# The sums of squares of the recurrence heads as two fp32r products, one unit later

## The reference

```
def _rmsnorm(x, g):
    xf = x.astype(jnp.float32)
    r = lax.rsqrt(jnp.mean(xf * xf, axis=-1, keepdims=True) + EPS)
    return (xf * r).astype(x.dtype) * g

_, o = lax.scan(_hgrn2_chunk_step, s0, xs)      # q, k, g, v in chunks of 64
o = o.transpose(1, 0, 3, 2, 4).reshape(B, S, HG_HEADS, HG_DV)
o = _rmsnorm(o, norm_g) * jax.nn.silu(og.reshape(B, S, HG_HEADS, HG_DV))

y = sigmoid(gate_a) * (a @ w_br_gm) + sigmoid(gate_b) * (b @ w_br_hg)    # a: gMLP branch, b: o
x = x + y @ w_out
x = x + _conv_ffn(_rmsnorm(x, ffn_norm), w_up, conv_w, conv_b, w_down)   # up 1024 -> 5632, down 2816 -> 1024
```

## Time and profile before

| | us |
|---|---|
| median of 3 runs | 2916.29 (2916.15 to 2920.58) |
| the profiled execution's own time | 2918.32 |
| its span, first to last instruction | 2916.5 |
| PE busy in the span | 2881.0 (99%) |
| DVE, ACT, POOL busy | 1459.5 (50%), 710.1 (24%), 195.8 (7%) |
| mean granted TensorE clock | 0.998 |

### The profile page before, as it was taken

The page is one execution under the profiler, slowest core; times in us unless marked ns, Lnnn a source line. Parts: engine busy times, 40 slices in busy tenths (PEclk is TensorE's granted clock), DMA queues, the critical chain, the costliest instruction groups (busy, mean ns, idle before and its releaser), DMA issues.

```text
span 2916.5 us, 33708 instructions
## 1 busy us (share of the span) xinstructions
PE 2881.0 (99%) x13472; PEld 2397.8 (82%) x13472; DVE 1459.5 (50%) x2870; ACT 710.1 (24%) x971; POOL 195.8 (7%) x87
## 2 busy tenths in 40 slices
PE   7999999999999999999999999999999999999998
PEld 6888888888888888888888888888888888888886
DVE  2886677755266434553325634455323563355521
ACT  3332244433122112221112211222111211122210
POOL 3323410014000000000000000000000000000000
PEclk9999999999999999999999999999999999999999
DMA  7657888889743465556564445555656345555554
GB/s 269 236 184 236 316 284 293 288 304 322 253 159 132 163 224 188 190 200 229 204 217 144 145 172 218 188 193 197 231 204 215 132 143 196 208 188 197 193 204 171
DMA packets 121979, 614.61 MB, mean 211 GB/s; under 512 B 13536, under 2 KB 13792, under 8 KB 74080
## 3 DMA queue, kind: packets, MB, share of 16 engines
q1 hardware_dynamic: 121824, 612.46, 59.8%
HBM read 474.00 MB, written 138.41 MB: 210 GB/s over the span
## 4 chain that ended last, share of the span: by engine, by line
PE 93%; DMA 2%; DVE 2%; issue 1%; POOL 1%; ACT 0%; SPq 0%; POOLq 0%; DVEq 0%; ACTq 0%
PE bank L889 26%; PE bank L890 26%; PE bank L894 26%; PE bank L950 3%; PE bank L937 2%; PE bank L938 2%; PE bank L939 2%; DMA w_split<-w_both 1%; POOL w_both L384 1%; DMA raw<-w_units 1%; PE bank L903 1%; PE bank L900 1%; PE bank L901 0%; PE bank L920 0%; PE bank L991 0%
## 5 line engine op out<-in xcount | busy, mean ns | idle before, releaser
L889 PE MATMUL bank<-h_hi,w_both 128*128 128x512 f32 x2400 | 945.5, 394 | 0.0
L890 PE MATMUL bank<-h_lo,w_both 128*128 128x512 f32 x2400 | 934.3, 389 | 0.0
L894 PE MATMUL bank<-h_hi,w_both 128*128 128x512 f32 x2400 | 593.5, 389 | 0.0
L890 PEld LDWEIGHTS bank<-h_lo,w_both 128*128 128x128 f32 x2400 | 450.7, 188 | 96.9 <-issue 4.8
L889 PEld LDWEIGHTS bank<-h_hi,w_both 128*128 128x128 f32 x2400 | 450.7, 188 | 96.9 <-issue 4.8
L894 PEld LDWEIGHTS bank<-h_hi,w_both 128*128 128x128 f32 x2400 | 450.5, 188 | 93.6
L811 DVE TENSOR_TENSOR z<-bank,rms_inv 128x512 f32<-128x512 f32 x176 | 121.8, 692 | 355.3 <-PE bank L894 347.7
L889 PE MATMUL bank<-g_hi,w_both 128*128 128x512 f32 x704 | 275.4, 391 | 0.0
L890 PE MATMUL bank<-g_lo,w_both 128*128 128x512 f32 x704 | 273.9, 389 | 0.0
L824 DVE SCALAR_TENSOR_TENSOR conv<-z,params,conv 128x512 f32<-128x512 f32 x352 | 263.7, 750 | 6.2
L384 POOL TENSOR_TENSOR w_both<-raw,w_both 128x1024 fp32r<-128x1024 f32 x80 | 194.7, 2434 | 531.4 <-ACT w_both L398 504.5
(11 more groups left out here) (187 smaller groups left out, 3055.4 us busy)
## 6 DMA issues: line engine op xcount, KB each, us to landing
w_both<-w_split SPq DMA_DIRECT2D x372, 1024.0 KB, 4.8
w_split<-w_both SPq DMA_DIRECT2D x248, 512.0 KB, 5.5
raw<-w_units SPq DMA_DIRECT2D x124, 512.0 KB, 5.3
x_in<-x_t SPq DMA_DIRECT2D x32, 256.0 KB, 5.5
res<-x_t SPq DMA_DIRECT2D x32, 256.0 KB, 5.1
out<-res SPq DMA_DIRECT2D x32, 256.0 KB, 6.8
masks<-masks_in SPq DMA_DIRECT2D x1, 1152.0 KB, 9.7
gm_w<-gm_wt SPq DMA_DIRECT2D x1, 256.0 KB, 6.9
```

The source lines that it names most:

```text
L889: pe.matmul(dst, w_hi[slot][:, off + k, :], rhs_hi(k), start=first and k == 0, stop=False)
L890: pe.matmul(dst, w_hi[slot][:, off + k, :], rhs_lo(k), start=False, stop=False)
L894: mm = pe.matmul(dst, w_lo[slot][:, off + k, :], rhs_hi(k), start=False, stop=last and k == n - 1)
```

## The change

The sum of squares over the channels becomes two fp32r matmuls of `ones_r` with the two halves of the squares: ScalarE makes the upper half (`sq_hi`, a copy behind the square), VectorE the rest (`sq_lo`, behind `a_lo`). Both halves lie where `sig_nf` and `sig_q` lay. TensorE issues the two matmuls behind the first unit of the next head, for the last head behind the first unit of the gates (`o_sum`). ScalarE takes the root there: behind `sig_nf` of the next head, or ahead of the first gate's sigmoid (`o_rms`); `sig_nf` itself waits for the sum, because it writes over `sq_hi`. VectorE finishes the head's output (`recurrence_out`, the five steps that stood at the head's end) between q0 and `qp1` of the next head, for the last head behind the loop. The steps get semaphores of their own.

```diff
--- before.py
+++ after.py
@@ -134,6 +134,7 @@
     masks = place("masks", [P, NC * P + len(LEVELS) * NC * P // 2], U32)
     ident = place("ident", [P, P])
     ones = place("ones", [P, P])
+    ones_r = place("ones_r", [P, P], F32R)
     eps = place("eps", [P, 1])
     scratch = place("scratch", [P, 8])
     gm_w = place("gm_w", [P, NH, P])
@@ -181,13 +182,14 @@
     SLOT = BLK + 64
     pool = room(10 * SLOT)
 
-    def temp(name, slot, width=TT):
-        return place(name, [P, width], F32, pool + slot * SLOT)
+    def temp(name, slot, width=TT, dt=F32):
+        return place(name, [P, width], dt, pool + slot * SLOT)
 
     sig_f, sig_nf, sig_q, sig_og = (temp(n, i) for i, n in enumerate(("sig_f", "sig_nf", "sig_q", "sig_og")))
     gm_mix, v_head = temp("gm_mix", 4), temp("v_head", 5)
     i_tok = place("i_tok", [P, NC, NH * P], F32, pool + 6 * SLOT)
     i_head = place("i_head", [P, TT])
+    sq_hi, sq_lo = (temp(n, i, dt=F32R) for n, i in (("sq_hi", 1), ("sq_lo", 2)))
     sum_n, diag_n = temp("sum_n", 1), temp("diag_n", 3)
     h_f32 = [temp("h_f32a", 4), temp("h_f32b", 5)]
     sq_r, diag_r = temp("sq_r", 6), temp("diag_r", 7)
@@ -207,6 +209,7 @@
     def sem(name):
         return nc.alloc_semaphore(name)
 
+    ones_made = sem("ones_made")
     par_in, consts_in, masks_here, res_in, out_sent = sem("par_in"), sem("consts_in"), sem("masks_here"), sem("res_in"), sem("out_sent")
     ident_here = sem("ident_here")
     x_next_in = [sem("x_next_in0"), sem("x_next_in1")]
@@ -219,14 +222,17 @@
     N_CONST = 16 * 3
 
     tok_act = Steps(sem("tok_act"), ["i0", "i1"] + [f"v{c}" for c in range(NC)])
-    head_act = Steps(sem("head_act"), ["i_head", "sig_f", "sig_q", "sig_og", "k_tok", "o_sq", "o_rms"])
-    head_pe = Steps(sem("head_pe"), ["s1", "diag", "k_tok", "s64_32", "s16_8", "s4_2", "update", "o", "mix", "o_sum"])
+    head_act = Steps(sem("head_act"), ["i_head", "sig_f", "sig_q", "sig_og", "k_tok"])
+    o_act = Steps(sem("o_act"), ["sq", "hi", "rms"])
+    o_dve = Steps(sem("o_dve"), ["lo", "inv", "unit", "b", "b_hi", "b_lo"])
+    o_pe = Steps(sem("o_pe"), ["sum"])
+    head_pe = Steps(sem("head_pe"), ["s1", "diag", "k_tok", "s64_32", "s16_8", "s4_2", "update", "o", "mix"])
     names = ["forget", "floor", "qp1"]
     for s in LEVELS:
         names += [f"qr{s}", f"qp{2 * s}", f"kl{2 * s}", f"kr{2 * s}", f"t{2 * s}"]
     head_dve = Steps(sem("head_dve"), ["k"] + names + [f"vh{c}" for c in range(NC)]
                      + ["m1", "m0", "m64", "m32", "m16", "m8", "m4", "m2", "st0", "st1", "st2", "st3", "st4",
-                        "mix", "a", "a_hi", "a_lo", "inv", "unit", "b", "b_hi", "b_lo"])
+                        "mix", "a", "a_hi", "a_lo"])
     ln_dve = Steps(sem("ln_dve"), [f"bn{c}" for c in range(NC)] + [f"ag{c}" for c in range(NC)] + ["inv"])
     ln_act = Steps(sem("ln_act"), ["std"])
     mix_dve = Steps(sem("mix_dve"), [f"{n}{j}" for j in range(2) for n in ("b", "a", "y", "y_hi", "y_lo")], 1)
@@ -449,6 +455,12 @@
             act.activation(spreads[:, 0, :], moments[:, :, 1], ACT.Sqrt, bias=eps[:, 0:1]).then_inc(*ln_act.did("std"))
             act.wait_ge(pro_dve, 8)
 
+            def o_rms(it):
+                act.wait_ge(*o_pe.at("sum", it))
+                act.wait_ge(*o_dve.at("lo", it))
+                act.activation(head_o[:, :], bank[5][:, :], ACT.Sqrt, bias=eps[:, 0:1],
+                               scale=1.0 / P).then_inc(*o_act.did("rms"))
+
             for h in range(0, NH):
                 it = t * NH + h
                 u = h * 6
@@ -456,7 +468,11 @@
                                ACT.Copy).then_inc(*head_act.did("i_head"))
                 unit_behind(t, U_HEAD, u)
                 act.activation(sig_f[:, :], bank[0][:, :], ACT.Sigmoid).then_inc(*head_act.did("sig_f"))
+                if h:
+                    act.wait_ge(*o_pe.at("sum", it - 1))
                 act.activation(sig_nf[:, :], bank[0][:, :], ACT.Sigmoid, scale=-1.0).then_inc(evac[0], 1)
+                if h:
+                    o_rms(it - 1)
                 unit_behind(t, U_HEAD + 1, u)
                 act.activation(sig_q[:, :], bank[1][:, :], ACT.Sigmoid).then_inc(*head_act.did("sig_q"))
                 unit_behind(t, U_HEAD + 2, u)
@@ -472,13 +488,14 @@
                 unit_behind(t, U_HEAD + 5, u)
                 act.activation(u_act[:, h, :], bank[1][:, :], ACT.Gelu).then_inc(evac[1], 1)
                 act.wait_ge(*head_pe.at("o", it))
-                act.activation(head_o[:, :], bank[4][:, :], ACT.Square).then_inc(*head_act.did("o_sq"))
-                act.wait_ge(*head_pe.at("o_sum", it))
-                act.activation(head_o[:, :], bank[5][:, :], ACT.Sqrt, bias=eps[:, 0:1],
-                               scale=1.0 / P).then_inc(*head_act.did("o_rms"))
+                act.activation(head_o[:, :], bank[4][:, :], ACT.Square).then_inc(*o_act.did("sq"))
+                act.wait_ge(*o_act.at("sq", it))
+                act.activation(sq_hi[:, :], head_o[:, :], ACT.Copy).then_inc(*o_act.did("hi"))
 
             for p in range(KD // 2):
                 unit_behind(t, U_MIX + 4 * p)
+                if p == 0:
+                    o_rms(t * NH + NH - 1)
                 act.activation(gate_a[NH + p], bank[0][:, :], ACT.Sigmoid).then_inc(evac[0], 1)
                 unit_behind(t, U_MIX + 4 * p + 1)
                 act.activation(gate_b[NH + p], bank[1][:, :], ACT.Sigmoid).then_inc(evac[1], 1)
@@ -594,7 +611,9 @@
         for steps in (mix_dve, out_dve, res_dve, pre_dve, fin_dve):
             dve.sem_inc(steps.sem, steps.head_start)
         dve.memset(sum_n[:, :], 0.0)
-        dve.memset(ones[:, :], 1.0)
+        dve.memset(ones[:, :], 1.0).then_inc(ones_made, 1)
+        dve.wait_ge(ones_made, 1)
+        dve.tensor_copy(ones_r[:, :], ones[:, :])
         dve.memset(eps[:, :], EPS).then_inc(pro_dve, 1)
         dve.wait_ge(pro_dve, 1)
         dve.wait_ge(par_in, 16)
@@ -651,6 +670,26 @@
             dve.wait_ge(*ln_act.at("std", t))
             dve.reciprocal(spreads[:, 1, :], spreads[:, 0, :]).then_inc(*ln_dve.did("inv"))
 
+            def recurrence_out(h):
+
+                it = t * NH + h
+
+                def then(name):
+                    dve.wait_ge(*o_dve.at(name, it))
+
+                dve.wait_ge(*o_act.at("rms", it))
+                dve.reciprocal(head_o[:, :], head_o[:, :]).then_inc(*o_dve.did("inv"))
+                then("inv")
+                dve.tensor_tensor(head_o[:, :], head_o[:, :], bank[4][:, :], ALU.mult).then_inc(*o_dve.did("unit"))
+                then("unit")
+                dve.scalar_tensor_tensor(out=head_o[:, :], in0=head_o[:, :], scalar=par_col(C_HGN), in1=og_act[:, :],
+                                         op0=ALU.mult, op1=ALU.mult).then_inc(*o_dve.did("b"))
+                then("b")
+                dve.tensor_scalar(b_hi[:, h, :], head_o[:, :], 1.0, None, ALU.mult).then_inc(*o_dve.did("b_hi"))
+                then("b_hi")
+                dve.tensor_tensor(b_lo[:, h, :], head_o[:, :], b_hi[:, h, :].bitcast(F32),
+                                  ALU.subtract).then_inc(*o_dve.did("b_lo"))
+
             for h in range(0, NH):
                 it = t * NH + h
                 used = t * B_TILE + h * 3 + B_HEAD
@@ -669,6 +708,8 @@
                 dve.wait_ge(*head_act.at("sig_q", it))
                 dve.tensor_tensor(q0[:, :], sig_q[:, :], bank[1][:, :], ALU.mult).then_inc(evac[1], 1)
                 then("floor")
+                if h:
+                    recurrence_out(h - 1)
                 dve.wait_ge(evac[1], used + 1)
                 dve.tensor_tensor(qp[:, :], q0[:, :], total[1][:, :], ALU.mult).then_inc(*head_dve.did("qp1"))
                 for s in LEVELS:
@@ -732,19 +773,9 @@
                 dve.tensor_tensor(a_lo[:, h, :], gm_mix[:, :], a_hi[:, h, :].bitcast(F32),
                                   ALU.subtract).then_inc(*head_dve.did("a_lo"))
 
-                dve.wait_ge(*head_act.at("o_rms", it))
-                dve.reciprocal(head_o[:, :], head_o[:, :]).then_inc(*head_dve.did("inv"))
-                then("inv")
-                dve.tensor_tensor(head_o[:, :], head_o[:, :], bank[4][:, :], ALU.mult).then_inc(*head_dve.did("unit"))
-                then("unit")
-                dve.scalar_tensor_tensor(out=head_o[:, :], in0=head_o[:, :], scalar=par_col(C_HGN), in1=og_act[:, :],
-                                         op0=ALU.mult, op1=ALU.mult).then_inc(*head_dve.did("b"))
-                then("b")
-                dve.tensor_scalar(b_hi[:, h, :], head_o[:, :], 1.0, None, ALU.mult).then_inc(*head_dve.did("b_hi"))
-                then("b_hi")
-                dve.tensor_tensor(b_lo[:, h, :], head_o[:, :], b_hi[:, h, :].bitcast(F32),
-                                  ALU.subtract).then_inc(*head_dve.did("b_lo"))
-
+                dve.wait_ge(*o_act.at("hi", it))
+                dve.tensor_tensor(sq_lo[:, :], head_o[:, :], sq_hi[:, :].bitcast(F32), ALU.subtract).then_inc(*o_dve.did("lo"))
```

(16 more changed lines are left out.)

## The result

The changed kernel takes 2975.88 us (median of 4 runs, 2973.67 to 2976.23), the kernel before 2917.08 in the same session: ratio 1.0195, 95% interval 1.018 to 1.0211. That is 59 us slower. 32 were forecast, and the time lies outside the range of 2935 to 2960.

A forecast was written before the change was run, and what follows sets the result against it. TensorE was taken as the bound, with VectorE already caught up in tile 0's heads. Terms 21.5 + 5.2 + 1.2 + 3.9 = +31.8 us gave 2950.1 on the profiled execution, 2948 as median; range 2935 to 2960.

The forecast's parts named there:

- Rival C: TensorE's clock falls after idling over 5 us in tile 0's three heads and gates: at most +9 us, 2957; chance 25%.
- Its table is loaded by then: Gates, tiles 1 to 3: root's table ready when the sum ends; TensorE waits 1.65, net loss 1.3 per tile, +3.9 us.
- Tile 0 up to the transposes: Heads 1 to 3 of tile 0: VectorE's chain is already last, so delays count in full; 7.2 per head, 21.5 us.
- the reload: Tile 0, ScalarE: sigmoid table loaded again behind the weights' copy; sig_q starts 2.37 after it, not 0.97: +1.40 per head.
- the three collisions of the forecast: Tile 0 heads: GpSimd's subtractions hold the product with the gate (+1.25) and levels twice (+2.2 each): 5.65, net +0.2.
- The gates of tile 0: Last head of tile 0: root's table load, the five steps and a GpSimd collision delay TensorE by 5.2; bounds 2.5 to 5.5.
- TensorE's own gain: Every head: the float32 sum matmul goes (0.83), two fp32r matmuls at 0.228 return; 0.37 gained per head, 6.0 us in all.
- the heads won 0.07 where they were to lose 0.14: Heads 1 to 3, tiles 1 to 3: moved steps delay the transposes, turning 0.37 gain into 0.14 loss; nine heads, +1.2 us.
- The wait for `level(1)`: Tile 0: part of TensorE's wait moves ahead to this point, about 1.4, inside the 7.2 per head.

The follow-up runs named there:

- work in the wait: Changed kernel plus 24 unread fp32r matmuls ahead of the wait for the transposes in heads 1 to 3 of tile 0: 2956.4 us, ratio 1.0132.
- two useless reciprocals: Kernel before plus two useless VectorE reciprocals (5.9 us) between q0 and qp1 in heads 1 to 3 of tile 0: 2953.98 us, ratio 1.0119.
- tile 0 alone: Kernel before with the change made in tile 0 only; tiles 1 to 3 keep the float32 sum and old order: 2964.5 us, ratio 1.0162.
- steps ahead of q0: Changed kernel with the five steps of the head's output ahead of q0 instead of behind it: 2966.61 us, ratio 1.0165.
- root first: Changed kernel; ScalarE's root waits for one semaphore and, at the gates, stands ahead of the first unit's wait: 2961.84 us, ratio 1.0146.
- one matmul: Kernel before with one fp32r matmul of the squares' upper half replacing the float32 one at the old place: 2907.98 us, ratio 0.996.
- TensorE's share: Kernel before with the sum as two fp32r matmuls of the same upper half at the old place: 2912.22 us, ratio 0.9982.
- the order that fits: Change's arithmetic with earlier sq_lo, sums inside the next head's first unit, output finished at the head's end; against kernel before: 2911.87 us, ratio 0.9974.

## Why the prediction was wrong

**Which step failed.** Rival C, as it was put: "at most 4 x 2.3 = +9 [...] behind the transposes come the small matmuls of the levels, which may hide it". The forecast's own sum had no term for the clock at all. The rival's bound was taken from the dense matmuls at the start, where the clock had come back after eleven of them. But the clock did not come back during the levels; each of the 48 short matmuls cost 0.20 instead of 0.11, and it rose only among the long matmuls of the next unit. One fall costs 6.7 in a head and not 2.3; three heads give 20.1, and the stretches behind the branches of tiles 0, 1 and 2, where the clock fell as well, grew by 0.7, 3.0 and 1.8. The run with work in the wait shows the 20 us, and the run with two useless reciprocals shows that a wait of 6 us from another cause brings them too. The forecast also gave the fall 25% where the waits were over 5 us long, and said that no gap but the first was long enough in the trace of before to show one. That was a misreading: at the program's end, behind two shorter waits with little work between, the clock of the kernel before is 0.50 as well (third row: the window, as above).
```profile
2903.75 1.05 PE L914 MATMUL bank<-ones,sum_r 128*128 128x1 f32 x8 [2.33 <-DVE sum_r L877]
2906.10 2.07 PE L920 MATMUL bank<-diag_r,ones 128*128 128x512 f32 x2 [1.29 <-DVE diag_r L563]
2908.00:2912.00 4.00, 0.17 (x1) 0.00 (x0) 3.79 (x6) 0.00 (x0) 0.00 (x0) 0.50 0.56 207
```
The Trainium skill's rule (TensorE: Matmul & The Clock Gate, HAM oscillation), quoted there as a rival, was the one that held: the traces agree, with a fall at each of the fifteen waits of 4.5 to 6.7 us in the heads.

**The second failure.** "Its table is loaded by then" at the gates of tiles 1 to 3. The load came 0.07 behind the sum, the wait for `b_lo` was 2.7 instead of 1.65, and the net loss 2.5 per tile and not 1.3: +3.5 us. In two of the three tiles the clock fell behind the longer wait, too.

**What held.** Tile 0 up to the transposes: 7.2 per head forecast, 6.5 to 6.6 measured. The rows of the changed kernel show the terms one by one, ScalarE first, with the reload between the copy of the weights and `sig_q`, 2.37 from start to start as worked out:
```profile
125.92 1.06 ACT L404 ACTIVATE w_both<-raw 128x1024 fp32r<-128x1024 f32 x1 [0.46 <-PE bank L925]
127.00 1.28 ACT L477 ACT_TABLE_LOAD   x1
128.29 0.60 ACT L477 ACTIVATE sig_q<-bank 128x512 f32<-128x512 f32 x1
```
The activation starts 0.01 behind the load, so again there is no drain of the kind that the Trainium skill (ScalarE: Activation LUTs, What ACT_TABLE_LOAD costs) adds to a switch. On VectorE the product with the gate is held by GpSimd (1.81 instead of 0.75), and so are two copies among the levels (2.46 and 2.43 instead of 0.29), each while GpSimd's subtraction runs (rows of POOL). These are the three collisions of the forecast, 5.4 in all where it had 5.65:
```profile
128.92 0.69 DVE L709 TENSOR_TENSOR q<-sig_q,bank 128x512 f32<-128x512 f32 x1 [4.03 <-ACT sig_q L477]
129.53 3.35 DVE L681 RECIPROCAL head_o<-head_o 128x512 f32<-128x512 f32 x1
...
132.50 2.39 POOL L390 TENSOR_TENSOR w_both<-raw,w_both 128x1024 fp32r<-128x1024 f32 x1 [3.04 <-ACT w_both L404]
133.63 1.81 DVE L685 SCALAR_TENSOR_TENSOR head_o<-head_o,params,og_act 128x512 f32<-128x512 f32 x1
...
136.55 0.68 DVE L714 TENSOR_TENSOR qp<-q,total 128x512 f32<-128x512 f32 x1
...
138.27 2.46 DVE L727 COPY kp<-kp 128x256 f32<-128x256 f32 x1
...
146.38 2.41 POOL L390 TENSOR_TENSOR w_both<-raw,w_both 128x1024 fp32r<-128x1024 f32 x1 [5.80 <-ACT w_both L404]
146.52 2.43 DVE L727 COPY kp<-kp 128x256 f32<-128x256 f32 x1
...
151.68 0.15 DVE L728 TENSOR_TENSOR total<-total 128x4 f32<-128x4 f32 x1
```
The gates of tile 0 lost 4.9 (forecast 5.2), and TensorE's own gain was 0.42 per head (forecast 0.37). In tiles 1 to 3 the weight load of the transposes waited 0.55 to 0.56 in each of the nine heads (forecast 0.51), and the heads won 0.07 where they were to lose 0.14. The wait for `level(1)` was 0.9 where 1.4 had been named. Without the clock and without the 3.5 us of the table, the places of the forecast's sum measured 19.7 + 4.9 + 7.4 - 3.5 - 0.6 = 27.9, against 31.8 put down.

**What stays open.** How long a wait brings the clock down is not settled. By the spacing of the matmuls behind them, the waits of 4.5 to 6.7 us in the heads did so fifteen times of fifteen (changed kernel, tile 0 alone, steps ahead of q0, useless reciprocals, root first) and those of 5.3 at the gates of tile 0 four times of four; the waits of 2.7 did so two times of three in the changed kernel and four of six in two others; the waits of 1.4 at the branches and of 1.25 to 1.28 at the transposes never. But of four waits of 1.7 to 2.1 for weights at the start of tile 1, two were followed by a fall (1.80 in the run with tile 0 alone, 1.76 in the run with one matmul) and two were not (1.72 in TensorE's share, 2.12 in the order that fits). In TensorE's share the clock also fell at 689.3, 2.4 us behind the start of short matmuls that had waited 1.03. Nor is it shown why a wait of one length does it once and not the next time. Of the 1.1 us behind the branches of tile 3, where the clock did not fall, no cause was found; the same stretch lies between 495.9 and 496.8 us in runs that change nothing in it.

## What to carry to other kernels

Before work is moved behind a step on a second engine, find the stage and tile in which that engine's chain already ends last; the delay counts there in full, however idle the engine is on average. Then price the wait with the clock: here each wait of over 4 us in the heads was followed by a stretch at half speed, which lasted through all 48 short matmuls and cost 6 to 7.5 us on top of the wait. The same arithmetic with the sum inside the next unit and the moved steps left at their place gained 7.5 us on the kernel before (2911.87 against 2919.38), where the change as made lost 59.

## What was not expected of the hardware

The clock, once at 0.50, stayed there through 9.8 us of back-to-back short matmuls (128 rows, 64 columns, float32), with TensorE's busy time at 5.00 of 5.00 in the windows, and in the changed kernel came back only after 5 to 12 matmuls of 512 columns more. Where the matmuls behind a wait were long from the start (the gates), 7 to 14 of them ran slowly, so the short ones had brought the clock back no sooner.
